# Turning the expert choice round: router weight columns held, tokens moving, constant products in TensorE's waits, and another order for the first expert's preparation

## The reference

```
probs = softmax(hf @ w_router)                # 256 x 8
vals, idx = top_k(probs, 2)
wts = vals / sum(vals)
combine = sum(one_hot(idx, 8) * wts[..., None], axis=1)
for e in range(8):
    gate, up = split(hf @ w_gu[e])            # 1024 -> 2 x 1792
    y = y + combine[:, e:e+1] * ((silu(gate) * up) @ w_down[e])
```

## Time and profile before

| | us |
|---|---|
| median of 3 runs | 1356.33 |
| lowest, highest | 1355.15, 1360.57 |
| profiled execution | 1354.17 |
| its span | 1352.4 |
| mean granted TensorE clock | 0.979 |

### The profile page before, as it was taken

How to read it: one execution, slowest core, us unless ns; L and a number is a source line. 1 busy time by engine, 2 the same in 40 slices (tenths; PEclk the granted TensorE clock), 3 DMA queues, 4 the chain that set the end, 5 groups by cost and what they waited for, 6 DMA issues and landing times.

```text
span 1352.4 us, 20422 instructions
## 1 busy us (share of the span) xinstructions
PE 1292.6 (96%) x7672; PEld 1133.0 (84%) x7672; DVE 1077.5 (80%) x1177; ACT 825.5 (61%) x1071; POOL 73.3 (5%) x103
## 2 busy tenths in 40 slices
PE   6989999999999999999989979999999999999996
PEld 5977999986988699998776768888889898989884
DVE  6888899896656677777665478888989898989888
ACT  5766666535556554443446547777777777776774
POOL 0020000003433000000002200000000000000000
PEclk9999999999999999999989969999999999999999
DMA  9945877589834389998432218999999999999991
GB/s 320 343 180 175 298 268 265 218 314 230 203 125 157 125 280 311 308 345 302 161 104 99 70 57 299 319 355 321 355 317 347 319 359 321 354 321 357 311 352 76
DMA packets 193035, 349.64 MB, mean 259 GB/s; under 512 B 23908, under 2 KB 161455, under 8 KB 186695
## 3 DMA queue, kind: packets, MB, share of 16 engines
q1 hardware_dynamic: 189713, 343.38, 74.0%
q10 hardware_dynamic: 2934, 4.24, 1.0%
q0 software_dynamic: 320, 1.08, 0.3%
HBM read 347.61 MB, written 1.06 MB: 258 GB/s over the span
## 4 chain that ended last, share of the span: by engine, by line
PE 85%; DVE 7%; ACT 6%; issue 2%; DMA 0%; POOL 0%; ACTq 0%; DVEq 0%
PE ps L1228 11%; PE ps L710 8%; PE ps L711 8%; PE ps L712 8%; PE ps L1198 8%; PE ps L1200 8%; PE ps L1199 8%; PE ps L723 5%; PE ps L727 5%; PE ps L725 5%; DVE wlo L1747 1%; ACT probs L1373 1%; PE ps L1169 1%; PE ps L1140 1%; PE ps L1176 1%
## 5 line engine op out<-in xcount | busy, mean ns | idle before, releaser
L1264 ACT ACTIVATE whi<-raw 128x1024 fp32r<-128x1024 f32 (+1 forms) x210 | 218.4, 1055 | 212.7 <-PE ps L712 135.2
L1747 DVE TENSOR_TENSOR wlo<-raw,whi 128x1024 fp32r<-128x1024 f32 (+1 forms) x210 | 255.5, 1239 | 101.9 <-ACT whi L1264 98.6
L710 PE MATMUL ps<-ahi,whi 128*128 128x256 f32 x976 | 282.0, 289 | 7.1 <-DVE alo L1779 6.7
L711 PE MATMUL ps<-alo,whi 128*128 128x256 f32 x976 | 278.6, 285 | 0.0
L712 PE MATMUL ps<-ahi,wlo 128*128 128x256 f32 x976 | 278.4, 285 | 0.0
L1754 DVE TENSOR_TENSOR wlo<-raw,whi 128x1792 fp32r<-128x1792 f32 (+1 forms) x96 | 199.9, 2090 | 25.1 <-ACT whi L1277 23.4
L1277 ACT ACTIVATE whi<-raw 128x1792 fp32r<-128x1792 f32 (+1 forms) x96 | 168.5, 1756 | 62.9 <-PE ps L1200 35.1
L710 PEld LDWEIGHTS ps<-ahi,whi 128*128 128x128 f32 x976 | 189.6, 194 | 12.3 <-issue 8.4
L711 PEld LDWEIGHTS ps<-alo,whi 128*128 128x128 f32 x976 | 189.9, 195 | 0.8 <-issue 0.7
L712 PEld LDWEIGHTS ps<-ahi,wlo 128*128 128x128 f32 x976 | 189.7, 194 | 0.0
L1198 PE MATMUL ps<-whi,hchi 128*128 128x448 f32 x352 | 131.6, 374 | 3.3 <-DVE hclo L2320 2.8
(11 more groups left out here) (334 smaller groups left out, 2514.7 us busy)
## 6 DMA issues: line engine op xcount, KB each, us to landing
raw<-in_moe_w_gu SPq DMA_DIRECT2D x96, 896.0 KB, 6.4
ada<-in_w_ada SPq DMA_DIRECT2D x48, 1024.0 KB, 6.8
raw<-in_moe_w_down SPq DMA_DIRECT2D x32, 1024.0 KB, 6.8
ada<-in_moe_w_gu SPq DMA_DIRECT2D x32, 896.0 KB, 6.4
raw<-in_w_up SPq DMA_DIRECT2D x22, 1024.0 KB, 5.2
raw<-in_ffn_w_gu SPq DMA_DIRECT2D x22, 1024.0 KB, 9.1
ada<-in_moe_w_down SPq DMA_DIRECT2D x16, 1024.0 KB, 7.0
raw<-in_na_w_qkv SPq DMA_DIRECT2D x12, 1024.0 KB, 7.4
```

The costliest lines, as they stand in the source:

```text
L710: pe.matmul(o, h[:, k, cols], bhi[:, k], start=(k == 0), stop=False)
L711: pe.matmul(o, h[:, k, cols], blo[:, k], start=False, stop=False)
L1264: act.activation(high_, src, ACT.Copy).then_inc(hi_done, 1)
L1747: ve.tensor_tensor(low_, src, high_.bitcast(F32), ALU.subtract).then_inc(lo_done, 1)
```

## The change

- Router: the 16 (or 8) columns of rt16 are held and the 256 tokens of ahi (alo) move; 16 matmuls. The logits come out with the experts on 16 partitions (8 high, 8 low halves). VectorE copies them to SBUF (lgT), TensorE multiplies lgT by a 16x8 matrix of two stacked identities (new constants C_SUM), which turns them and adds the halves, and VectorE copies the result.
- fill(3, 2) on TensorE between the turned logits and the wait for chosen; fill(3, 1) between totals and the gather.
- VectorE: row_lo(1) behind chosen; behind make_pick(0) come split_expert(0), gathered(1), gathered_lo(0), and only then the weights' sum and the list of passes with experts_known. gathered_lo(1) and the other splits stay behind it.
- ScalarE: split_expert(0) at the end of norm(5), ahead of split_expert(1); the rounding of the first four feature tiles (gathered_hi0) ahead of its own modulation.
- values_made becomes a second count of keys_made; the router weights' DMA releases router_in itself, by 16, in place of an increment by GpSimd. These free semaphores for the two new ones.

The functions gathered and gathered_lo only move up in the program; their bodies are as they were.

```diff
@@ -133,7 +133,8 @@
 C_HOT = C_EID + 8
-C_ALL = C_HOT + S
+C_SUM = C_HOT + S
+C_ALL = C_SUM + NE
@@ -169,6 +170,7 @@
     c[bucket, C_HOT + np.arange(S)] = 1.0
+    c[0:2 * NE, C_SUM:C_SUM + NE] = np.tile(np.eye(NE), (2, 1))
     return c
@@ -417,6 +419,7 @@
         wcol = u("wcol", NT * 12).rearrange("p (t n) -> p t n", t=NT)
+        lgT = u("lgT", S, parts=2 * NE)
         eidf = u("eidf", 16)
@@ -1071,7 +1074,7 @@
                 if t == 0:
-                    m.then_inc(sem("values_made"), 1)
+                    m.then_inc(sem("keys_made"), 1)
             done(m)
@@ -1107,16 +1110,20 @@
                     pe.wait_ge(sem("aT_ready"), AT0[5] + k // 2 + 1)
-                for t in range(NT):
-                    tok = slice(t * P, t * P + P)
-                    o = ps[:, 4 + t, 0:2 * NE]
-                    if k < KT - 1:
-                        pe.matmul(o, ahi[:, k, tok], rt16[:, k], start=(k == 0), stop=False)
-                    m = pe.matmul(o[:, 0:NE], alo[:, k, tok], rt16[:, k, 0:NE], start=False, stop=False)
-                    if k == KT - 1:
-                        m = pe.matmul(o, ahi[:, k, tok], rt16[:, k], start=False, stop=True)
+                o = ps[0:2 * NE, 4, 0:S]
+                if k < KT - 1:
+                    pe.matmul(o, rt16[:, k], ahi[:, k], start=(k == 0), stop=False)
+                m = pe.matmul(o[0:NE], rt16[:, k, 0:NE], alo[:, k], start=False, stop=False)
+                if k == KT - 1:
+                    m = pe.matmul(o, rt16[:, k], ahi[:, k], start=False, stop=True)
             m.then_inc(sem("logits"), 1)
+            pe.wait_ge(sem("logits_copied"), 1)
+            for t in range(NT):
+                m = pe.matmul(ps[:, 5, t * NE:(t + 1) * NE], lgT[:, t * P:(t + 1) * P], cst[0:2 * NE, C_SUM:C_SUM + NE],
+                              start=True, stop=True)
+            m.then_inc(sem("logits_turned"), 1)
+            fill(3, 2)
             pe.wait_ge(sem("chosen"), 1)
@@ -1124,6 +1131,7 @@
             pe.matmul(ps[:, 4, 0:2 * NE], ones, sel, start=True, stop=True).then_inc(sem("totals"), 1)
+            fill(3, 1)
@@ -1650,9 +1658,9 @@
             down(W_MLO, 4, 1)
-            act.wait_ge(sem("router_in"), 1)
+            act.wait_ge(sem("router_in"), 16)
             act.activation(rt16[:, :, 0:NE], rtr.rearrange("p (k e) -> p k e", k=KT), ACT.Copy).then_inc(sem("router_hi"), 1)
-            norm(5, lambda q: None if q else split_expert(0), lambda q: split_expert(1) if q else None, sc_f, sh_f)
+            norm(5, lambda q: None, lambda q: (split_expert(0), split_expert(1)) if q else None, sc_f, sh_f)
@@ -1673,8 +1681,14 @@
+                gathered_hi0(count)
+                gathered_hi1(count)
+            def gathered_hi0(count):
                 act.wait_ge(sem("hc_f32"), count)
                 act.activation(hchi[:, 0:4], hc[:, 0:4], ACT.Copy).then_inc(sem("hc_hi"), 1)
+            def gathered_hi1(count):
                 act.wait_ge(sem("hc_high"), count)
@@ -1684,8 +1698,9 @@
+            gathered_hi0(1)
             gathered(1)
-            gathered_hi(1)
+            gathered_hi1(1)
             split_expert(2)
@@ -2195,7 +2210,7 @@
             latent_low(1, 0, 2)
-            ve.wait_ge(sem("values_made"), 1)
+            ve.wait_ge(sem("keys_made"), 2)
             values(0)
@@ -2223,13 +2238,11 @@
             norm(5, lambda q: None, lambda q: None, sc_f, sh_f, residual_gate(4, W_MOE), lambda: row_lo(0))
-            row_lo(1)
             ve.wait_ge(sem("logits"), 1)
-            lg = ps[:, 4:6, 0:2 * NE].rearrange("p t (two e) -> p t two e", two=2)
+            ve.tensor_copy(lgT, ps[0:2 * NE, 4, 0:S]).then_inc(sem("logits_copied"), 1)
             logit = rw[:, 16:18, :]
-            own.link(ve.tensor_copy(rw[:, 18:20, :], lg[:, :, 1]))
-            own.link(ve.tensor_tensor(logit, lg[:, :, 0], rw[:, 18:20, :], ALU.add))
+            ve.wait_ge(sem("logits_turned"), 1)
+            own.link(ve.tensor_copy(logit, ps[:, 5, 0:2 * NE].rearrange("p (t e) -> p t e", t=NT)))
             ve.tensor_reduce(nmx[:, 0, :], logit, AXX, ALU.max, negate=True).then_inc(sem("router_max"), 1)
@@ -2248,10 +2261,7 @@
             ve.wait_ge(sem("chosen"), 1)
-            ve.wait_ge(sem("router_exp"), NT)
-            own.link(ve.tensor_tensor(wts, rw[:, 0:2, :], chosen, ALU.mult))
-            own.link(ve.tensor_reduce(rsum[:, 1, :], wts, AXX, ALU.add))
-            own.link(ve.reciprocal(rsum[:, 2, :], rsum[:, 1, :]))
+            row_lo(1)
@@ -2265,7 +2275,31 @@
+            def gathered(count, first=False):
...
+            def gathered_lo(half, n):
...
+                ve.tensor_tensor(hclo[:, k], hc[:, k], hchi[:, k].bitcast(F32), ALU.subtract).then_inc(sem("hc_ready"), 1)
             make_pick(0)
+            split_expert(0)
+            gathered(1, True)
+            gathered_lo(0, 1)
+            ve.wait_ge(sem("router_exp"), NT)
+            own.link(ve.tensor_tensor(wts, rw[:, 0:2, :], chosen, ALU.mult))
+            own.link(ve.tensor_reduce(rsum[:, 1, :], wts, AXX, ALU.add))
+            own.link(ve.reciprocal(rsum[:, 2, :], rsum[:, 1, :]))
             own.link(ve.tensor_tensor(wts, wts, rsum[:, 2, :].rearrange("p (t o) -> p t o", o=1).broadcast_to(full), ALU.mult))
@@ -2302,23 +2336,6 @@
-            def gathered(count, first=False):
...
-            def gathered_lo(half, n):
...
-                ve.tensor_tensor(hclo[:, k], hc[:, k], hchi[:, k].bitcast(F32), ALU.subtract).then_inc(sem("hc_ready"), 1)
             def down_lo(p):
@@ -2334,9 +2351,6 @@
             ve.sem_inc(sem("pickT_ready"), 1)
-            gathered(1, True)
-            split_expert(0)
-            gathered_lo(0, 1)
             gathered_lo(1, 2)
@@ -2439,10 +2453,9 @@
             po.dma_start(rtr.rearrange("p (k e) -> p k e", k=KT), a["moe_w_router_2"][0].rearrange("(k p) e -> p k e", p=P))\
-                .then_inc(sem("router_dma"), 16)
+                .then_inc(sem("router_in"), 16)
             po.dma_start(final_scale, a["final_norm_2"].rearrange("(o n) -> o n", o=1).broadcast_to([P, D])).then_inc(sem("final_in"), 16)
-            po.wait_ge(sem("router_dma"), 16)
-            po.sem_inc(sem("router_in"), 1)
+            po.wait_ge(sem("router_in"), 16)
...
```

More of the change, by code:

```diff
@@ L2266, in make_pick @@
                 m.then_inc(sem("pick_ready"), 1)
-            make_pick(0)
+            def gathered(count, first=False):
+                if first:
+                    ve.wait_ge(sem("gathered_first"), 1)
+                else:
+                    ve.wait_ge(sem("gathered_turned"), count)
+                for k in range(4):
+                    m = ve.tensor_scalar(hc[:, k], ps[:, 6, k * P:(k + 1) * P], sc_f[:, k:k + 1], sh_f[:, k:k + 1],
+                                         ALU.mult, ALU.add)
+                m.then_inc(sem("hc_f32"), 1)
+            def gathered_lo(half, n):
+                k = slice(4 * half, 4 * half + 4)
+                ve.wait_ge(sem("hc_hi"), n)
+                ve.tensor_tensor(hclo[:, k], hc[:, k], hchi[:, k].bitcast(F32), ALU.subtract).then_inc(sem("hc_ready"), 1)
+            make_pick(0)
+            split_expert(0)
[5 more added lines that the diff above has]
+            own.link(ve.reciprocal(rsum[:, 2, :], rsum[:, 1, :]))
             own.link(ve.tensor_tensor(wts, wts, rsum[:, 2, :].rearrange("p (t o) -> p t o", o=1).broadcast_to(full), ALU.mult))
@@ L2303, in _ @@
             ve.tensor_copy(eidi, eidf).then_inc(sem("experts_known"), 1)
-            def gathered(count, first=False):
[L2307 to L2314, removed]
-            def gathered_lo(half, n):
-                k = slice(4 * half, 4 * half + 4)
-                ve.wait_ge(sem("hc_hi"), n)
-                ve.tensor_tensor(hclo[:, k], hc[:, k], hchi[:, k].bitcast(F32), ALU.subtract).then_inc(sem("hc_ready"), 1)
             def down_lo(p):
```

## The result

| | before | after |
|---|---|---|
| median | 1355.95 us | 1349.15 us |
| lowest, highest | 1355.15, 1360.57 | 1348.24, 1350.79 |
| profiled execution, its span | 1354.17, 1352.4 | 1349.48, 1347.7 |
| mean granted clock | 0.979 | 0.979 |

The ratio is 0.9947, 95% interval 0.9931 to 0.9962: 6.8 us faster (five executions on each side).

The account below looks back on a forecast made before the run. TensorE-bound expert passes were taken as unchanged, so the first expert matmul's start decides: 813.3 against 812.74, with experts_known replacing hclo, +0.55 us. That gave 1354.7 for the profiled execution, 1357 us as median, range 1352.6 to 1361.5.

Parts of the forecast that it names:

- part 4: VectorE and ScalarE order: hc_ready 5.7 us earlier, but TensorE waits for experts_known; first expert matmul 813.3, +0.55 us.
- the first paragraph: What bounds the kernel: eight TensorE-bound expert passes, left alone; only the start and clock of the first expert matmul can move.
- Part 1: Router with tokens moving: 16 matmuls for 32, last group from 794.05, VectorE starts at 795.3, 2.8 us earlier.
- the gap: TensorE's idle 2.35 us ahead of the router matmuls, in which the granted clock was expected to fall to half.
- A clock that is full through the router: Listed sign that the forecast was wrong; the clock was expected at half through the router stage.
- Part 2: Turning and summing the logits: copy 0.40 us, turned logits at 797.0, maximum 1.35 us earlier, choice at 798.9.
- Part 3: Constant products in waits: place count about 800.2, clock back at full by then, gather from 802.2 taking 3.5 us.
- the one in which hc_ready decides: Rival at the first expert matmul: it starts at 807.1, -5.7 us, 1350.6 us; chance 0.03.
- The half-clock case: Rival: clock stays at half until the experts, first expert matmul 816.7, +4.0 us, 1360.3 us; chance 0.24.
- the full-clock case: Rival: clock never falls from the router on, -1.3 us, 1355.0, or 1352.7 if held through later idle; chance 0.18.
- no load was missed: Rival: expert loads issued 3 us later are felt in the first pass, +3 us, 1360 us; chance 0.03.

Follow-up runs that it names:

- b_pad8: Kernel before with 8 unused columns at the end of the constants table, no instruction edited; 1348.17 us, ratio 0.9948 to before.
- a_again: The changed kernel run once more, nothing altered; 1347.77 us, ratio 0.9935 to before.
- a_nofill: The changed kernel without fill(3, 2) and fill(3, 1), its three constant products; 1349.66 us, ratio 0.9942 to before.
- a_listfirst: The changed kernel with VectorE's list of passes, up to experts_known, back ahead of the first rows' gathering; 1345.20 us, ratio 0.9922 to before.
- a_spread: The changed kernel with VectorE reordered towards experts_known and ScalarE's half of chunk 0 back where it was before; 1344.28 us, ratio 0.9914 to before.
- a_pad8: The changed kernel with 8 further unused constant columns, buffers behind them again off the boundary; 1359.68 us, ratio 1.0038; repeated, 1353.92 us, 0.9992.
- b_pad8_again: Kernel before with 8 unused columns at the end of the constants table, second measurement; 1348.35 us, ratio 0.9932 to before.

## Why the prediction was wrong

**The step that failed** is the end of part 4: "the 8 further constant columns: nothing". I priced them as a DMA and as a load's readiness and did not ask what lies behind the table in SBUF. Practically all of the 6.8 us is theirs: the same 8 columns in the unedited kernel gave 7.4 and, the second time, 7.6. With it fell the first paragraph's "the change leaves them alone" of the passes.

**The terms.** Between 846.3 and the last pass the changed kernel gains 4.4 us in seven passes: 84 down matmuls of 6 ns less each give 3.5, gate and up 0.9. The latter could give up to 0.37 us a pass (39.8 to 39.45 for 192), but in the changed kernel's profile most passes stay at 39.8; in b_pad8's all are at 39.45. The earlier stages have held operands behind the table too. The down-projection of one feed-forward layer (L723 to L727) took 61.67 us before and 60.29 after for 264 matmuls, and the first 48 of the other 10.96 and 10.68; at full clock throughout that would be an estimated 2.7 us in all. In the profiled pair it doesn't show at 777 us. The granted clock between 600 and 700 us was 0.98 before and 0.93 after:

```profile
600.00:700.00 100.00, 93.91 (x476) 79.10 (x474) 67.60 (x71) 38.63 (x55) 0.90 (x1) 0.93 0.59 211
```

4.4 + 2.7 = 7.1 fits the medians, 6.8 and 7.4 for b_pad8, but that the 2.7 reaches them is not shown. Over all profiles the last norm's residual starts at 774.5 to 779.0 us in the eight with these operands on the boundary and at 776.2 to 783.7 in the six with them off it, a difference of the middle values of 0.9.

**It could have been seen before.** The trace of before holds both steps side by side. ahi lies ahead of the table, and the output projection that holds it stepped, at full clock and with the same 512 columns moved:

```profile
776.77 0.62 PE L723 MATMUL ps<-whi,ahi 128*128 128x512 f32 x2
777.23 0.62 PE L725 MATMUL ps<-wlo,ahi 128*128 128x512 f32 x2
777.68 0.61 PE L727 MATMUL ps<-whi,alo 128*128 128x512 f32 x2
778.13 0.62 PE L723 MATMUL ps<-whi,ahi 128*128 128x512 f32 x2
```

Six matmuls in 1.36 us, 227 ns each, while the down-projection with gchi stepped by 234. These matmuls with ahi step by a mean of 228 in all fourteen traces, wherever the buffers behind the table lie.

**Where it was right.** Part 1: the last group started at 794.48 (forecast 794.05) and the copy at 795.57 (795.3). The clock, though, fell later than I had it, at about 793.5 and not in the gap; the first eight router matmuls stepped by 0.12 us. A clock that is full through the router was to be a sign of being wrong; full for half of it, it changed nothing here. In a_again it fell in the gap, and the copy starts 17.77 us after the residual in both, since the third group waits for alo either way and the last runs on behind it at half clock. Part 2: the copy 0.41 (0.40), the logits back at 797.09 (797.0), the choice 799.04 (798.9). What the Trainium skill gives for a read of PSUM (VectorE: DVE Perf Modes, section on the fixed latency per instruction), an estimated 0.39, agrees with the 0.41. Part 3: places 800.45 (800.2), gather 802.17 (802.2); a_nofill confirms both the price and what it buys. Part 4: rows gathered from 804.21 (804.15), hc_ready 806.97 (806.95), experts_known 811.79 (811.9), first expert load at 813.74 (813.8), first expert matmul 813.09 (813.3). By a_listfirst and a_spread the wait for experts_known is what took the place of the wait for hclo: aimed at, it gives 1.5 and 3.2 us, or 1.9 and 3.6 at equal clock.

**The rivals.** None of them named the mechanism. The measured time came nearest to the one in which hc_ready decides (1350.6), and would have seemed to prove it; the trace has the first expert matmul 6 us after hc_ready. The half-clock case fell with the clock back at the place count, the full-clock case with the clock at half from 793.5 until then, and no load was missed: the first chunk loaded late was issued 3 us later, as said, and ScalarE took up its splits at 825.59 as before (825.53).

## What to carry to other kernels

An edit that adds a buffer or widens a table also moves everything allocated behind it, and that part acts on stages that no line of the diff names: compare steps of one shape in different stages of the trace before calling it free, and time the padding by itself. Keep the starts of held operands in such matmuls at multiples of 512 bytes from a buffer that steps fast, as here; 32 bytes beside one cost 6 ns of 227 in the down-projection. Whether 64 would do wasn't tried. When a wait is removed, list all that the waiting engine is queued for; here the next one, the list of small operations with the register load behind it, was done 6 us later and took the whole gain of this stage.

## What the runs showed of the hardware

For fp32r matmuls with 128 columns held at full clock, the step depended on where the held operand starts: for 512 columns moved 227 ns on the boundary and 233 ns 32 bytes to either side of it; for 448 a median of 203 ns on it, 204 past it and 206 ahead of it, but with means that overlap (204.8 in the changed kernel and in a_pad8). At half clock no such difference was seen: the first chunk's steps were 0.37 us either way.

The same idle time of TensorE ahead of the router, 2.34 to 2.35 us, left the granted clock at half in some profiles (before, a_again) and full for 2 us more in others (after, b_pad8_again).

Why aligned gate and up matmuls still step by 207 ns in some chunks of some passes (a pass is 64.75 or 65.08 us), and from what size of boundary on a start counts as aligned, was not tried.
